# Two RMS norms rewritten: HGRN's root applied behind its projections, the final norm's weights applied during the down units

## The chip, the cores and the metric

One core of a Trainium2 chip runs the whole program. The metric is the device time of one execution in microseconds (us), here the median of a few runs. One execution was also taken by the hardware profiler, which is where the rows further down come from. Matmuls of TensorE (PE) are issued one behind the other; a PE that is busy in every slice is the bound of that slice.

## The reference

The input x is 512 tokens by 1024 features. Block one: `h = x`; HGRN2 mixer, feed-forward (FFN), dilated attention, FFN, each behind an RMS norm and added to h; block two: a sparse attention and gated linear attention mixer, FFN, and a last norm. What the change touches:

```python
def rmsnorm(x, gain):
    y = x * lax.rsqrt(jnp.mean(x * x, axis=-1, keepdims=True) + NORM_EPS)
    return y * gain

u = rmsnorm(h, norm_mix[0])
q, f, i, g = split(u @ w_in)            # four projections for each of 8 heads
forget = lb + (1 - lb) * sigmoid(f);  key = 1 - forget;  query = silu(q);  value = i
...                                     # chunked recurrence, decays from log(forget)
o = rmsnorm(o, out_gain) * silu(g)
...
return rmsnorm_2(x, norm_final)
```

The root `rsqrt(...)` is one number for each token, so `(x * gain * root) @ w` is the same as `((x * gain) @ w) * root`.

## The kernel before, in words

**Layout.** Activations are feature-major: h is eight chunks of 128 features by 512 tokens, float32. The input of a section is split into a rounded high part and a low part (`us`, u_split), as are the weights (`ws`, w_split), and a unit of projection is 24 matmuls: eight chunks by three products (high by high, low by high, high by low, lines 383 to 385), into one PSUM bank.

**Weights.** SP's DMA queue brings each unit's weights into a ring of 4 slots (line 306 for the first four, line 316 later, each when the unit four places earlier has been used). ScalarE (ACT) rounds them into one of 2 slots of w_split (`hi`, line 1013), which it can do once PE has used the unit two places earlier, and GpSimd (POOL) makes the low part (`lo`, line 1495). PE's unit waits for that low part. So each engine's queue, written out by hand, sets when weights are ready: a `hi` that stands behind a waiting instruction comes late.

**The start.** SP loads x (line 298), then gains and ones (line 300), then four units of weights, then the other constants. ACT squares the eight chunks (line 1024), VectorE (DVE) adds the squares (line 1713), PE sums them over the partitions with a matrix of ones (lines 396 and 398, `mean_square`), ACT makes the root from Ln and Exp (lines 1084 and 1086, `rms`). Then DVE multiplies each chunk by gain and root (line 1700), ACT rounds it (line 1034), and POOL (even chunks, line 1504) and DVE (odd chunks, line 1694) make the low part. PE's unit 0 follows that chunk by chunk. Units 0 to 3 are f, q, g, i of head 0, units 4 and 5 are f and q of head 1. Then head 0 begins with its transposes (line 533).

**A head.** ACT takes the sigmoids of f, q and g straight from PSUM (`hgrn_sigmoid`, line 1153) and copies i (`hgrn_value`, line 1161). DVE makes forget, key and query (`hgrn_gates`, lines 1923 to 1927; the query product reads q from PSUM), and silu of g (line 1931, from PSUM). ACT's Ln (line 1157), DVE's scan (line 1826) and the differences of levels (lines 1835, 1836, 1841) lead to ACT's Exp (`decay_exps`, line 1125) and POOL's products with keys and queries (`decayed`, lines 1564, 1565, 1558), between which POOL makes the low parts of the weights of two units. While PE works on one head, the other engines prepare the next, and PE's projections for the next heads are placed between its score matmuls. `FREED` names the semaphore by which a projection's bank becomes free. At a head's end DVE multiplies the output by gain and gate (line 1881), and, after ACT's root for that head, by the root (line 1893).

**The end.** After the last FFN's down units (h is updated on DVE, lines 1771 and 1774) the sum of squares goes as at the start; then `norm(7)` has DVE multiply the eight chunks by gain and root (line 1700) and ACT issues a DMA for each (line 1483).

## Time and profile before

| | |
|---|---|
| runs | 2269.19, 2271.11, 2276.2 us; median 2271.11 |
| the profiled execution | 2268.27 us; span of the core 2266.5 us |
| mean granted clock of PE | 0.987 of full speed |
| busy, share of the span | PE 96%, DVE 44%, ACT 39%, POOL 52% |
| DMA | 193.30 MB, mean 85 GB/s |

The span is 1.8 us shorter than the execution's own time. PE's share is high in nearly all of 40 slices of the page; the first slice is the exception (4 tenths, granted clock 8 tenths), and a smaller one is the last (7 tenths). A timeline row gives the start, the duration, the engine, the line, the operation, what it writes and reads, a count where rows are merged, and in brackets how long the engine sat idle before it and what released it.

### The profile page before, as it was taken

To read this page: it belongs to the slowest core of one execution; us is meant where nothing else is said; L and a number is where in the kernel's file an instruction comes from. 1 tells how busy PE (TensorE), PEld (TensorE's weight loads), DVE (VectorE), ACT (ScalarE), POOL (GpSimd) and SP (SyncE) were. 2 spreads that over 40 slices of the span, in tenths; PEclk is the share of its full clock that TensorE was granted. 3 is DMA by queue.
4 is the path that set the end of the run, shared out by engine and by line. 5 is a ranking of instruction groups with operands and counts; after the bars stand their busy time and mean duration, and the time that the engine had idled before them with its cause. 6 is when DMAs were issued, how large, how long until landed. Compare 5 with 4: busy or idle time off the path is not lost. (4 is left out here: it accounts for less than half of the span.)

```text
span 2266.5 us, 28352 instructions
## 1 busy us (share of the span) xinstructions
PE 2180.3 (96%) x10458; PEld 1795.5 (79%) x10458; DVE 1007.2 (44%) x1479; ACT 872.8 (39%) x1237; POOL 1175.6 (52%) x639
## 2 busy tenths in 40 slices
PE   4899999999999999989999999999899999999997
PEld 3788878888888978878888888788656888888886
DVE  5365566431434037754431446442675235422432
ACT  4567754221323223444221333434465234322222
POOL 3877855554565454535554555455113555554552
PEclk8999999999999999999999999999899999999999
DMA  3121213332332322223332332322101223332331
GB/s 135 56 65 56 74 47 93 93 109 86 95 108 85 93 85 67 72 70 102 94 112 83 93 107 88 123 63 90 56 14 51 95 93 93 100 110 80 101 104 72
DMA packets 53254, 193.30 MB, mean 85 GB/s; under 512 B 6816, under 2 KB 7728, under 8 KB 52912
## 3 DMA queue, kind: packets, MB, share of 16 engines
q1 hardware_dynamic: 50688, 184.95, 26.1%
q10 hardware_dynamic: 2480, 7.19, 0.8%
q8 instruction: 56, 0.92, 0.2%
q14 instruction: 30, 0.25, 0.0%
HBM read 187.92 MB, written 4.19 MB: 85 GB/s over the span
## 5 line engine op out<-in xcount | busy, mean ns | idle before, releaser
L1495 POOL TENSOR_TENSOR w_split<-ring,w_split 128x1024 fp32r<-128x1024 f32 (+3 forms) x327 | 842.9, 2578 | 857.1 <-ACT w_split L1013 857.1
L1013 ACT CAST w_split<-ring 128x1024 fp32r<-128x1024 f32 (+3 forms) x327 | 356.4, 1090 | 1018.2 <-PE ps L385 882.8
L383 PE MATMUL ps<-u_split,w_split 128*128 128x512 f32 x1768 | 705.8, 399 | 22.5 <-POOL w_split L1495 9.7
L385 PE MATMUL ps<-u_split,w_split 128*128 128x512 f32 x1768 | 693.3, 392 | 0.0
L384 PE MATMUL ps<-u_split,w_split 128*128 128x512 f32 x1768 | 692.9, 392 | 0.0
L383 PEld LDWEIGHTS ps<-u_split,w_split 128*128 128x128 f32 x1768 | 334.9, 189 | 102.0 <-issue 19.9
L385 PEld LDWEIGHTS ps<-u_split,w_split 128*128 128x128 f32 x1768 | 334.6, 189 | 71.5
L384 PEld LDWEIGHTS ps<-u_split,w_split 128*128 128x128 f32 x1768 | 335.0, 189 | 68.3 <-issue 1.2
L383 PE MATMUL ps<-hid,w_split 128*128 128x512 f32 x648 | 254.5, 393 | 4.2 <-DVE arena L1975 2.8
L384 PE MATMUL ps<-hid,w_split 128*128 128x512 f32 x648 | 253.3, 391 | 0.0
L385 PE MATMUL ps<-hid,w_split 128*128 128x512 f32 x648 | 253.1, 391 | 0.0
L1790 DVE TENSOR_TENSOR arena<-arena 128x512 f32<-128x512 f32 x66 | 161.9, 2454 | 66.1 <-ACT arena L1101 66.1
L1788 DVE TENSOR_TENSOR arena<-ps,rs_norm 128x512 f32<-128x512 f32 x66 | 45.6, 691 | 261.2 <-PE ps L385 239.2
L383 PEld LDWEIGHTS ps<-hid,w_split 128*128 128x128 f32 x648 | 122.4, 189 | 30.6 <-DVE arena L1975 3.2
L385 PEld LDWEIGHTS ps<-hid,w_split 128*128 128x128 f32 x648 | 122.3, 189 | 25.5
L384 PEld LDWEIGHTS ps<-hid,w_split 128*128 128x128 f32 x648 | 122.4, 189 | 25.4 <-issue 0.2
L1771 DVE TENSOR_TENSOR arena<-arena,ps 128x512 f32 x28 | 19.3, 688 | 187.5 <-PE ps L385 187.5
L1564 POOL TENSOR_TENSOR arena<-arena 128x256 f32<-128x256 f32 x70 | 62.5, 893 | 48.2 <-ACT arena L1125 48.2
L1531 POOL TENSOR_TENSOR hid<-arena,hid 128x512 f32 (+1 forms) x66 | 85.2, 1291 | 4.2 <-ACT hid L1105 4.2
L474 PEld LDWEIGHTS ps<-arena 128*128 128x128 f32 (+1 forms) x672 | 80.5, 190 | 6.7 <-issue 3.7
L1794 DVE TENSOR_TENSOR arena<-ps,rs_norm 128x512 f32<-128x512 f32 x66 | 45.6, 691 | 80.9 <-PE ps L385 80.9
L474 PE MATMUL ps<-arena 128*128 128x64 f32 (+1 forms) x672 | 81.4, 271 | 0.0
(297 smaller groups left out, 2535.6 us busy)
## 6 DMA issues: line engine op xcount, KB each, us to landing
ring<-in_w_hgrn SPq DMA_DIRECT2D x32, 512.0 KB, 3.6
ring<-in_w_attn_qk SPq DMA_DIRECT2D x24, 512.0 KB, 3.5
ring<-in_w_merge SPq DMA_DIRECT2D x24, 512.0 KB, 3.2
ring<-in_w_gu0a SPq DMA_DIRECT2D x22, 512.0 KB, 3.5
ring<-in_w_gu0b SPq DMA_DIRECT2D x22, 512.0 KB, 3.6
ring<-in_w_gu1a SPq DMA_DIRECT2D x22, 512.0 KB, 3.5
ring<-in_w_gu1b SPq DMA_DIRECT2D x22, 512.0 KB, 3.5
ring<-in_w_gu2a SPq DMA_DIRECT2D x22, 512.0 KB, 3.5
```

What stands on the lines that cost most here:

```text
L383: nc.tensor.matmul(ps[:, bank], ws[:, 0, r, w], act[:, 0, c], start=c == 0, stop=False)
L384: nc.tensor.matmul(ps[:, bank], ws[:, 0, r, w], act[:, 1, c], start=False, stop=False)
L385: m = nc.tensor.matmul(ps[:, bank], ws[:, 1, r, w], act[:, 0, c], start=False, stop=c == n - 1)
L474: m = nc.tensor.matmul(ps[:, 4 + n % 2, at:at + C // 2], dv[rows, l, t], later_half, start=True, stop=True)
L1013: nc.scalar.copy(ws[:, 0, slot, 0:w], ring[:, r, 0:w]).then_inc(s["w_hi"], 1)
L1495: nc.gpsimd.tensor_tensor(ws[:, 1, slot, 0:w], ring[:, r, 0:w], ws[:, 0, slot, 0:w].bitcast(F32), ALU.subtract).then_inc(s["w_lo"], 1)
L1531: nc.gpsimd.tensor_tensor(dst, gtmp[:, j % 2], src.bitcast(F32), ALU.subtract).then_inc(s["g_lo"], 1)
L1564: nc.gpsimd.tensor_tensor(x[:, :, 0], x[:, :, 0], kk[:, :, 0], ALU.mult)
L1771: nc.vector.tensor_tensor(hj, hj, ps[:, base + j], ALU.add).then_inc(s["h_ready"], 1)
L1788: nc.vector.tensor_tensor(gnorm[:, x], ps[:, 2 * x], rs[:], ALU.mult).then_inc(s["gate_norm"], 1)
L1790: nc.vector.tensor_tensor(sgate[:, x], sgate[:, x], gnorm[:, x], ALU.mult).then_inc(s["gate_silu"], 1)
L1794: nc.vector.tensor_tensor(gtmp[:, x], ps[:, 2 * x + 1], rs[:], ALU.mult).then_inc(s["up_norm"], 1)
```

## The change

- **Loads.** Gains and the logits of the lower bound come first, then unit 0's weights, then x with one semaphore for each pair of chunks, then ones, the next three units of weights, and the other constants.
- **HGRN's input.** `first_norm` on ACT and `first_input` on DVE make the high part as `h * gain` (ACT, Copy with a scale) and the low part as `h * gain - high` (DVE), without the root, and the squares in between. POOL has no part in it. PE runs unit 0 before the sum of squares.
- **The root.** `hgrn_raw` on DVE multiplies each projection in PSUM by the root (`rs`) and writes it to SBUF: four products a head, 32 in all. Sigmoids then read SBUF; the query and silu products have two SBUF operands; ACT's copy of i is gone. A projection's bank is free after `hgrn_raw`.
- **Places in a head.** The sigmoid of g moves to the head's start on ACT, silu behind the first level on DVE (`prepare(1)`, not `prepare(0)`), and the raw products stand at a head's end on DVE.
- **The last norm.** `last_input` on DVE makes `h * gain` for all chunks and the square of the last chunk during the down units (into `h_gained`); `last_norm` multiplies by the root in five products (1, 1, 2, 2 and 2 chunks), each with one DMA.
- Several semaphores are merged (for example four `mix_*` into `mix_steps`), with the same waits.

```diff
-            for c in range(DC):
-                sp.dma_start(h[:, c], a["x"][:, c]).then_inc(s["x_loaded"], 16)
-            for dst, name in constants[:2]:
-                sp.dma_start(dst[:], a[name]).then_inc(s["norm_consts"], 16)
...
+                    for dst, const in constants[:2]:
+                        sp.dma_start(dst[:], a[const]).then_inc(s["norm_consts"], 16)
+                    sp.dma_start(ring[:, 0, 0:width], w[0]).then_inc(w_ready[0], 16)
+                    for c in range(DC):
+                        sp.dma_start(h[:, c], a["x"][:, c]).then_inc(s[f"x_loaded{c // 2}"], 16)
+                    sp.dma_start(ones[:], a["ones"]).then_inc(s["norm_consts"], 16)
+                    for k in range(1, RING):
...
-            FREED = ("sig_f", "query", "silu_g", "vf_ready")
+            FREED = ("raw_f", "raw_q", "raw_g", "vf_ready")
...
-            pe.wait_ge(s["norm_consts"], 32)
+            hgrn_project(0, 0, ready=u_chunk(0))
+            pe.wait_ge(s["norm_consts"], 16 * 3)
             mean_square(0)
-            for k in range(4):
-                hgrn_project(0, k, ready=None if k else u_chunk(0))
+            for k in range(1, 4):
+                hgrn_project(0, k)
...
+            def first_norm():
+                act.wait_ge(s["norm_consts"], 16 * 2)
+                hi("hgrn", 0)
+                for c in range(DC):
+                    act.wait_ge(s[f"x_loaded{c // 2}"], 16 * 2)
+                    nc.scalar.activation(us[:, 0, c], h[:, c], ACT.Copy, scale=gains[:, 0, c:c + 1]).then_inc(s["u_hi"], 1)
+                    if c >= 4:
+                        act.wait_ge(s["sq_sum"], max(c - 4, 1))
+                    nc.scalar.activation(nsq[:, c % 4], h[:, c], ACT.Square).then_inc(s["sq_ready"], 1)
+                hi("hgrn", 1)
+                hi("hgrn", 2)
+                rms(0)
...
+            def first_input(c):
+                dve.wait_ge(s["u_hi"], c + 1)
+                nc.vector.scalar_tensor_tensor(out=us[:, 1, c], in0=h[:, c], scalar=gains[:, 0, c:c + 1],
+                                               in1=us[:, 0, c].bitcast(F32), op0=ALU.mult, op1=ALU.subtract
+                                               ).then_inc(s["u_lo_odd"] if c % 2 else s["u_lo_even"], 1)
+                if c >= 2:
+                    add_square(0, c - 1)
...
+            def hgrn_raw(head, done, bank, dst):
+                unit = (1, 0, 2, 3).index(bank)
+                dve.wait_ge(s["w_used"], cnt(head, 4, FIRST["hgrn"] + unit + 1))
+                nc.vector.tensor_tensor(dst, ps[:, bank], rs[:], ALU.mult).then_inc(s[done], 1)
...
-            lo("hgrn", 0)
-            norm(0, "hgrn")
-            lo("hgrn", 2)
-            lo("hgrn", 3)
-            hgrn_decayed(0, {4: lambda: lo("hgrn", 4), 8: lambda: lo("hgrn", 5)})
-            lo("hgrn", 6)
+            for k in range(5):
+                lo("hgrn", k)
+            hgrn_decayed(0, {2: lambda: lo("hgrn", 5), 5: lambda: lo("hgrn", 6)})
             lo("hgrn", 7)
...
+            def last_input(n, j):
+                if j == DC - 1:
+                    dve.wait_ge(s["h_ready"], h_done(NORM_AFTER[n], j))
+                    nc.vector.tensor_tensor(nsq[:, 3], h[:, j], h[:, j], ALU.mult).then_inc(s["sq_ready"], 1)
+                for c in {4: (0, 1), 5: (2, 3), 6: (4, 5), 7: (6, 7)}[j]:
+                    dve.wait_ge(s["h_ready"], h_done(NORM_AFTER[n], c))
+                    nc.vector.tensor_scalar(h_gained[:, c], h[:, c], gains[:, n, c:c + 1], None, ALU.mult
+                                            ).then_inc(s["u_tmp"], 1)
```

The order on ACT in the start, from the squares to the weights of unit 5. Before (`arena` with `128x1024` and `128x1536` are the decays, `w_split` is a `hi`):

```order
L1084 ACTIVATE rs_norm<-ps,small 128x512
L1086 ACT_TABLE_LOAD
L1086 ACTIVATE rs_norm<-rs_norm 128x512
L1034 CAST u_split<-arena 128x512 x4
L1013 CAST w_split<-ring 128x1024
L1034 CAST u_split<-arena 128x512 x4
L1153 ACT_TABLE_LOAD
L1153 ACTIVATE arena<-ps 128x512
L1013 CAST w_split<-ring 128x1024
L1153 ACTIVATE arena<-ps 128x512
```

and now:

```order
L1020 CAST w_split<-ring 128x1024 x2
L1093 ACT_TABLE_LOAD
L1093 ACTIVATE rs_norm<-ps,small 128x512
L1095 ACT_TABLE_LOAD
L1095 ACTIVATE rs_norm<-rs_norm 128x512
L1172 ACTIVATE arena<-arena 128x24
L1020 CAST w_split<-ring 128x1024
L1160 ACT_TABLE_LOAD
L1160 ACTIVATE arena<-arena 128x512 x2
L1169 ACT_TABLE_LOAD
L1169 ACTIVATE arena<-arena 128x512
L1020 CAST w_split<-ring 128x1024
```

The weights of units 1 and 2 are rounded ahead of the root, those of unit 3 ahead of the sigmoids, those of unit 4 behind Ln.

DVE from one head's end to the next head's scan, in the loop over heads. Before:

```order
L1881 SCALAR_TENSOR_TENSOR arena<-ps,small,arena 128x512 [waits o_sq,o_lo]
L1892 REGISTER_ALU [waits o_scaled]
L1893 TENSOR_TENSOR arena<-arena 128x512 [waits o_rstd]
L1853 REGISTER_ALU
L1854 TENSOR_TENSOR arena<-ps,ident_sb 128x512 [waits score_ps]
L1944 REGISTER_ALU
L1931 TENSOR_TENSOR arena<-arena,ps 128x512 [waits sig_g,scores]
```

and now, up to the same place:

```order
L1893 TENSOR_TENSOR arena<-ps,rs_norm 128x512 [waits w_used]
L1878 SCALAR_TENSOR_TENSOR arena<-ps,small,arena 128x512 [waits o_sq,silu_g,o_lo]
L1892 REGISTER_ALU [waits o_scaled]
L1893 TENSOR_TENSOR arena<-ps,rs_norm 128x512 [waits w_used]
L1892 REGISTER_ALU
L1893 TENSOR_TENSOR arena<-ps,rs_norm 128x512 [waits w_used]
L1886 ISA [waits o_scaled]
L1887 TENSOR_TENSOR arena<-arena 128x512 [waits o_rstd]
L1892 REGISTER_ALU
L1893 TENSOR_TENSOR arena<-ps,rs_norm 128x512 [waits w_used]
L1849 REGISTER_ALU
L1850 TENSOR_TENSOR arena<-ps,ident_sb 128x512 [waits score_ps]
```

Four products with the root (now line 1893) stand around the head's output, and the silu product has left the place behind line 1850.

## Rows read from the trace of the kernel before

**Rows 1.** Windows: busy us of engines, PEclk, DMA share, GB/s in a stretch.
```profile
54.00:56.00 2.00, 1.86 (x5) 1.50 (x6) 2.00 (x7) 0.59 (x1) 0.09 (x1) 0.60 0.21 84
93.00:118.00 25.00, 25.00 (x139) 21.30 (x138) 11.62 (x19) 19.14 (x24) 23.46 (x20) 1.00 0.27 85
```
**Rows 2.** Source line 298, the loads of x.
```profile
DMA to landing us min/median/max: 2.9/4.1/5.5
```
**Rows 3.** Timeline, the start up to the end of unit 0.
```profile
9.62 1.28 ACT L1024 ACT_TABLE_LOAD   x1 [9.62 <-DMA arena<-in_x]
10.92 4.27 ACT L1024 ACTIVATE arena<-arena 128x512 f32<-128x512 f32 x8
...
15.09 1.03 ACT L1013 CAST w_split<-ring 128x1024 fp32r<-128x1024 f32 x1
...
16.93 2.05 PE L396 MATMUL ps<-arena,ones_sb 128*128 128x512 f32 x2 [16.93 <-DVE arena L1713]
...
23.24 2.08 DVE L1700 SCALAR_TENSOR_TENSOR arena<-arena,gains_sb,rs_norm 128x512 f32<-128x512 f32 x3 [4.25 <-ACT rs_norm L1086]
...
26.59 0.77 PE L383 MATMUL ps<-u_split,w_split 128*128 128x512 f32 x1 [6.05 <-POOL u_split L1504]
...
40.19 0.60 ACT L1153 ACTIVATE arena<-ps 128x512 f32<-128x512 f32 x1 [1.39 <-PE ps L385]
```
**Rows 4.** Timeline, units 2 to 5 and the start of head 0.
```profile
50.73 1.22 DVE L1826 TENSOR_TENSOR_SCAN arena<-reset_sb,arena 128x512 f32<-128x512 f32 x1
51.45 2.64 POOL L1495 TENSOR_TENSOR w_split<-ring,w_split 128x1024 fp32r<-128x1024 f32 x1 [7.25 <-ACT w_split L1013]
...
54.14 0.58 PE L383 MATMUL ps<-u_split,w_split 128*128 128x512 f32 x1 [2.74 <-POOL w_split L1495]
...
56.64 3.30 POOL L1564 TENSOR_TENSOR arena<-arena 128x256 f32<-128x256 f32 x1 [2.55 <-ACT arena L1125]
...
58.65 0.68 DVE L1841 TENSOR_TENSOR arena<-arena 128x512 f32<-128x512 f32 x1
...
67.17 0.77 PE L383 MATMUL ps<-u_split,w_split 128*128 128x512 f32 x1 [5.68 <-POOL w_split L1495]
...
75.15 1.28 POOL L1558 TENSOR_TENSOR arena<-arena 128x512 f32<-128x512 f32 x1
75.33 0.47 PE L383 MATMUL ps<-u_split,w_split 128*128 128x512 f32 x1 [0.43 <-POOL w_split L1495]
...
80.88 0.60 PE L533 MATMUL ps<-ident_sb,arena 128*128 128x128 f32 x4
...
94.63 0.48 ACT L1205 COPY arena<-ps 128x384 f32<-128x384 f32 x1 [1.03 <-PE ps L546]
```
**Rows 5.** Page, costliest groups: busy us, mean ns of one | idle before.
```profile
L1790 DVE TENSOR_TENSOR arena<-arena 128x512 f32<-128x512 f32 x66 | 161.9, 2454 | 66.1 <-ACT arena L1101 66.1
L1788 DVE TENSOR_TENSOR arena<-ps,rs_norm 128x512 f32<-128x512 f32 x66 | 45.6, 691 | 261.2 <-PE ps L385 239.2
```
**Rows 6.** Timeline of POOL and of PE, inside the loop over heads.
```profile
157.91 0.77 POOL L1564 TENSOR_TENSOR arena<-arena 128x256 f32<-128x256 f32 x1 [6.47 <-ACT arena L1125]
...
172.28 2.38 POOL L1495 TENSOR_TENSOR w_split<-ring,w_split 128x1024 fp32r<-128x1024 f32 x1
...
173.88 1.02 PE L500 MATMUL ps<-arena,ones_sb 128*128 128x512 f32 x2
```
**Rows 7.** Timeline, the last norm.
```profile
2253.18 0.68 DVE L1713 TENSOR_TENSOR arena<-arena 128x512 f32<-128x512 f32 x1
...
2253.91 1.13 PE L396 MATMUL ps<-arena,ones_sb 128*128 128x512 f32 x2 [1.38 <-DVE arena L1713]
...
2254.88 1.02 PE L398 MATMUL ps<-arena,ones_sb 128*128 128x512 f32 x2
...
2258.60 5.39 DVE L1700 SCALAR_TENSOR_TENSOR arena<-arena,gains_sb,rs_norm 128x512 f32<-128x512 f32 x8 [4.74 <-ACT rs_norm L1086]
2259.38 4.98 ACTq L1483 DMA_DIRECT2D out_h<-arena  x8
```

More of the change, by code:

```diff
@@ L1013, in hi, with last_norm @@
                 nc.scalar.copy(ws[:, 0, slot, 0:w], ring[:, r, 0:w]).then_inc(s["w_hi"], 1)
[L1015 to L1021 removed]
+            def last_norm(n):
+                for c in range(DC - 1):
+                    act.wait_ge(s["h_ready"], h_done(NORM_AFTER[n], c))
                     if c >= 4:
@@ L1145, in _, with hgrn_sigmoid, hgrn_gate_sigmoids @@
             act.wait_ge(s["credit"], 2)
-            norm(0, "hgrn")
-            def hgrn_sigmoid(head, k, dst, done):
-                src = (1, 0, 2)[k]
-                act.wait_ge(s["w_used"], cnt(head, 4, FIRST["hgrn"] + k + 1))
-                if head != 0 and k:
-                    act.wait_ge(s[("", "query", "silu_g")[k]], cnt(later(head, -1), 1, 1))
-                nc.scalar.activation(dst, ps[:, src], ACT.Sigmoid).then_inc(s[done], 1)
+            first_norm()
+            def hgrn_sigmoid(head, raw, src, dst, done):
+                act.wait_ge(s[raw], cnt(head, 1, 1))
+                nc.scalar.activation(dst, src, ACT.Sigmoid).then_inc(s[done], 1)
+            def hgrn_gate_sigmoids(head):
+                hgrn_sigmoid(head, "raw_f", sf_, sf_, "sig_f")
+                hgrn_sigmoid(head, "raw_q", qry[(head if isinstance(head, int) else head[1]) % 2], sq_, "sig_q")
             def hgrn_log(head):
@@ L1479, in _ @@
             ffn(2, None)
-            norm(7)
-            for c in range(DC):
-                act.wait_ge(s["credit"], 3 + c)
-                act.dma_start(out[:, c], h[:, c]).then_inc(s["stored"], 16)
-            act.wait_ge(s["stored"], 16 * DC)
+            last_norm(7)
+            for n, (lo, hi) in enumerate(LAST_PARTS):
+                act.wait_ge(s["credit"], 3 + n)
+                act.dma_start(out[:, lo:hi], h[:, lo:hi]).then_inc(s["stored"], 16)
+            act.wait_ge(s["stored"], 16 * len(LAST_PARTS))
         @block.gpsimd
@@ L1772, in residual @@
                 for j in range(loops, DC):
+                    for c in {6: (1, 2, 3, 4), 7: (5, 6)}.get(j, ()):
+                        add_square(norm, c)
                     dve.wait_ge(s["w_used"], FIRST[section] + j + 1)
                     nc.vector.tensor_tensor(h[:, j], h[:, j], ps[:, base + j % 2], ALU.add).then_inc(s["h_ready"], 1)
-                    for c in {5: (1, 2, 3), 6: (4, 5), 7: (6,)}.get(j, ()):
-                        add_square(norm, c)
+                    if norm is not None:
+                        last_input(norm, j)
             def ffn(f, norm):
@@ L1819, in _ @@
             nc.vector.memset(start[:, 2:3], 0.0).then_inc(s["o_rstd"], 2)
-            for c in range(1, DC - 1):
-                add_square(0, c)
-            dve.wait_ge(s["norm_consts"], 32)
+            for c in range(DC):
+                first_input(c)
             def cumulate(it, b, log_decay):
@@ L1886, in head_output @@
                     return
-                if head != HEADS_H - 2:
-                    output_rooted(head, r, tmp, dst, done)
             def output_rooted(head, r, tmp, dst, done):
@@ L1962, in hgrn_head @@
                     end_exponents(bcum, dec)
+                    hgrn_raw(nxt, "vf_ready", 3, vf)
                 dve.wait_ge(s["o_lo"], cnt(head, 1, 1))
                 head_output(head, hgain, ors, otmp, sgl, otmp, s["o_full"])
+                if more:
+                    dve.wait_ge(s["o_scaled"], cnt(head, 1, 1))
+                    hgrn_raw(nxt, "raw_g", 2, sgl)
+                if not isinstance(head, int):
+                    hgrn_raw(nxt2, "raw_f", 1, sf_)
+                    output_rooted(head, ors, otmp, otmp, s["o_full"])
+                    hgrn_raw_query(nxt2)
             over_heads(dve, hgrn_head)
@@ L2346, in _ @@
             ffn(2, 7)
-            norm(7, s["credit"])
+            last_norm(7, s["credit"])
 def kernel(**inputs):
```

158 lines of the change are left out of this document (62 added, 96 removed).

## The prediction

> **What bounds the kernel now.** I read the windows first. From the first heads on PE is busy for all of a stretch (25.00 of 25.00 us) at a granted clock of 1.00 [rows 1]: work of DVE, ACT or POOL taken away there is worth nothing, unless it ends a wait of PE. So the edit can only pay in the first 80 us and the last 15 us, and can only hurt by a new wait in between. Next I read the timeline of the start. PE does its first projection matmul at 26.59 us, after x has landed (9.62), eight squares, their sum, a sum over partitions from 16.93, the root, the products and the low parts; unit 0, held up chunk by chunk, is done at 40.19, where the sigmoid that reads it starts [rows 3]. Units 1 to 5 follow with three waits for low parts of weights (2.74, 5.68 and 0.43 us), and head 0 starts at 80.88 [rows 4]. PE's work in these units is small: unit 5 takes 80.88 - 75.33 = 5.55 us at full clock [rows 4]. The clock matters too: right after the idle 2.74 us the granted clock was 0.60 over the stretch 54 to 56 [rows 1]. Unit 3 ran from 54.14 to 61.49 (67.17 less 5.68), 7.35 us, or 1.8 more than unit 5, and unit 4 from 67.17 to 74.90, 7.73 us, or 2.2 more [rows 4]. PE is then at the lower of its two levels, 1.2 GHz, and climbs back to 2.4 after some microseconds of work.
>
> **The change, part by part: the new start.**
> - First work. Unit 0's weights are now the third DMA, issued near 1.7 us. A transfer of x took 2.9 to 5.5 us to land [rows 2]; I take 3.5, so 5.2 us. ACT: table load (1.28) beforehand, rounding 1.03 [rows 3], to 6.3. POOL's low part, 2.4 to 2.6 [rows 4, 6], to 8.8. PE starts at 8.8 and not at 26.59.
> - Pace of unit 0. ACT spends a product (0.6) and a square (4.27 / 8 = 0.53) per chunk, 1.15 us; DVE a low part (2.08 / 3 = 0.69 [rows 3]) and an add (0.68 [rows 7]), 1.4 with gaps. PE at 1.2 GHz needs 3 x 0.427 = 1.28 us a chunk (512 columns at 1.2 GHz). All three end near 19: ACT finishes chunk 7 at 16.6, DVE at 18.6, PE at 19.0. x itself is not the limit: it landed at 9.62 and now has 0.57 MB more ahead of it, about 11, and ACT reaches the last pair at 14.
> - Sum of squares, now behind unit 0: 2.0 us at full clock [rows 7], 3.6 at half, since its first half alone took 2.05 in the start [rows 3]. PE will have worked for 10 us by then, so I take 2.0: 21.0. Its price is new on PE; the root's latency is hidden behind unit 1.
> - Units 1 to 3. The rounding of unit 1 is done at 17.6, its low part at 20.3; unit 2's at 22.7. They run back to back to 26.5, 32.0 and 37.5. Unit 3's rounding waits for the end of unit 1, 26.5, and is ready at 30.1, before 32.0.
> - The log of forget. ACT after that rounding (27.6): table load 1.28, two sigmoids of 0.60 [rows 3], table load, Ln 0.6: 32.0. Unit 4's rounding needs unit 2 done (32.0), so it ends at 33.1, its low part at 35.7 (2.64 [rows 4]), in time for 37.5. Unit 4 ends at 43.0.
> - Unit 5's low part is the late one. DVE's scan to the last difference took 50.73 to 59.33 = 8.6 us [rows 4], so now 32.1 to 40.7. POOL's first decay product was held for 3.30 us, to 59.94, 0.6 behind DVE's last difference [rows 4]; so here it ends at 41.3. Three more halves of 0.72 bring 43.5, and the low part of unit 5, which now stands behind two levels, 45.9. Its rounding, behind ACT's third Exp, is ready before. PE idles 2.9 us and pays 1.8 for the clock as unit 3 did: unit 5 ends at 53.2.
> - Head 0 thus starts at 53.2 instead of 80.88: **-27.7 us**. What it needs next is ready: keys and queries at 31, the value at 42, POOL's decays by 58, while PE's transposes of them were over 94.6 - 80.9 = 13.7 us into the head [rows 4], now 67.
>
> Bounds. Were unit 0's weights to land 2 us later, the sum of squares to take 3.6 and unit 1 to run low (2.2), it is 5.8 us less: -21.9. Were POOL's first product not held, it is up to 2.6 us of idle and 1.8 of clock more: -32.1.
>
> **The heads.** DVE gets four products a head from PSUM: line 1788 is the same form and takes 0.691 us, so 32 x 0.69 = 22 us, of which DVE's idle time takes all as long as nothing PE waits for is behind them. ACT loses the copy of i and two table loads a head, worth nothing while PE is busy. The products at a head's end wait for projections that PE has issued before the matmul that DVE's next step needs, so they hold nothing up. The tight place is elsewhere: POOL's second low part ends at 172.28 + 2.38 = 174.66, and PE, whose two ones-matmuls start at 173.88 and take 0.86 together, needs it at about 174.75 [rows 6]: 0.1 us of slack. That chain starts with Ln, which now stands behind a third sigmoid (0.6), and with the scan, which stands behind silu (0.69); against this ACT has lost a copy and two table loads on the way there, about 0.4 us of it before the sigmoids by my estimate. I take 0; the upper bound is 0.65 x 6 heads = +4 us. A gain is excluded, since PE has no idle time there.
>
> Two products change sides, though: query and silu read PSUM before and now have two SBUF operands. Line 1790, with two SBUF operands beside a busy POOL, takes 2.454 us; line 1788, with one, 0.691 [rows 5]. At the place where query and silu stand (some 4 us into a head) POOL waits for the decays, 6.47 us in all [rows 6], so I price them at 0.7 each. The Trainium skill (SBUF — State Buffer, "SBUF: two separate sides") says that VectorE instructions with two SBUF inputs and GpSimd's share a port pair as an exclusive lock for the whole instruction. By it the raw products, with one SBUF input, cost POOL nothing, and the two moved ones can wait for a whole low part; the trace agrees in the two means. It is the mechanism of the slower rival.
>
> **The end.** Now: DVE's last add (2253.18, 0.68), then four matmul halves from 2253.91 to 2255.9, then the root [rows 7]. In the change the adds are over before the last update, so the first pair of halves (1.0) runs before it, and DVE's square of chunk 7 (0.68) takes the place of the add; only the second pair follows: **-1.0 us**. The last products take 2 x 0.67 + 3 x 1.21 = 5.0 instead of 5.39 [rows 7], but the eight transfers, issued from 2259.38 and landed at 2266.5 (2.1 MB in 7.1 us), already keep pace with DVE; I count 0 of that 0.4. Bounds -1.4 and 0. The gain products (0.6 each) lie beside down units of over 7 us.
>
> **Sum.** 2268.27 - 27.7 + 0 - 1.0 = 2239.6 against the profiled execution. The median of the runs shown is 2.8 us above it, which would make 2242.4. I take **2241**. A change of this kernel's time can be told from none beyond 0.3%, or 6.8 us.
>
> **The rivals.**
> 1. *Part of it is given back.* The start comes in at the upper bounds, and the loop slips by half a microsecond a head. For it: 0.1 us of slack [rows 6], and the clock, which fell after only 2.74 us of idle. Against it: in each head PE's other waits have microseconds of slack. 2241 + 5.8 + 4 gives up to 2251.
> 2. *The start was covered anyway.* If head 0, reached early, waits for POOL's decays, the gain moves from the norm to there. POOL took 76.4 - 56.6 = 19.8 us for them [rows 4]; from 37.9 that is 57.7, while PE needs them at 66. To eat the gain, POOL would have to be some 30 us later. The same goes for late loads. 2262 or more.
> 3. *Slower: query and silu queue behind POOL.* If both are held as line 1790 is, each costs 2.454 - 0.69 = 1.76 us more; with 0.6 of the third sigmoid and 0.69 of the moved silu the scan is 4.8 us later in every head, POOL's decays with it, and PE waits 4.7 us for a low part in 6 to 7 heads, each time with 1.8 for the clock: 6.5 x 7 = 45 us, 2241 + 45 = 2286. It makes the kernel slower by 0.3% from about 4 us of delay a head. Against it: POOL's 6.47 us without work at this place of every head [rows 6].
>
> **How the numbers follow.** My forecast 0.78, rival 1 0.13, rival 2 0.04, rival 3 0.05. The first two are faster by over 0.3%, and some 0.01 of the second rival: faster 0.92, same 0.03, slower 0.05. The forecast's own bounds are 2241 - 4.4 - 0.4 = 2236 and 2241 + 5.8 + 1 = 2248; with rival 1, and 2 us for the spread between runs, the range is 2234 to 2252.
>
> **What would show it.** Right: PE's first projection matmul near 9 us, unit 0 over by 20, one wait of about 3 us before unit 5, head 0 (line with the transposes) near 53; no idle time of PE inside the loop; only two matmul halves between the last update and Ln. Wrong: an idle row of PE before the second low part of a head, releaser POOL, in every head (rival 1 or, if over 4 us, 3); query or silu products at about 2 us; a wait of PE on POOL's decays in head 0 (rival 2); half clock from 20 to 30 us. If PE's first matmul is not before 15 us, the step on the loads is wrong.

## The result, and the profile after

| | before | after |
|---|---|---|
| runs, us | 2269.19, 2271.11, 2276.2, 2277.68 | 2245.87, 2254.36, 2254.52, 2254.84 |
| median, us | 2273.65 | 2254.44 |
| the profiled execution, time / span, us | 2268.27 / 2266.5 | 2254.36 / 2252.6 |
| mean granted clock, profiled execution | 0.987 | 0.987 |
| busy: PE, DVE, ACT, POOL | 96, 44, 39, 52% | 97, 46, 38, 52% |

The ratio (of the means) is 0.9906, with a 95% interval from 0.9883 to 0.9929: the kernel is faster, by some 19 us between the medians and 21 us between the means. Before now has a fourth run (2277.68), which the forecast did not have. One later run of before, 2787.31 us at a granted clock of 0.745, is left out of all comparisons below. The forecast was 2241 us (2234 to 2252), so the direction was right and the size was not; the result is above the range.

Where the two profiled executions part is read best from the times at which PE reaches the same place in both:

| PE reaches | before | after | gained so far |
|---|---|---|---|
| transposes of head 0 | 80.88 | 53.38 | 27.5 |
| transposes of head 1 | 114.01 | 90.05 | 24.0 |
| first lone matmul of the output units | 321.58 | 300.32 | 21.3 |
| last norm, the ones-matmuls behind the last chunk | 2253.91 | 2240.79 | 13.1 |
| end of the span | 2266.5 | 2252.6 | 13.9 |

So 27.5 us were gained by head 0, 3.5 given back in head 0, 2.7 in the later heads, 8.1 in the 1940 us behind them, which the change does not touch, and 0.8 gained at the end. A "lone" matmul is the first one behind the heads that waits for POOL's product of the output units (line 521 before, 527 after); it marks the end of all that the start and the heads do.

**The start** came nearly as worked out. The timeline of after, from the first unit's weights to head 0 (start, duration, engine, line, operation; idle before it and its releaser):

```profile
6.75 1.04 ACT L1020 CAST w_split<-ring 128x1024 fp32r<-128x1024 f32 x1
7.87 2.35 POOL L1496 TENSOR_TENSOR w_split<-ring,w_split 128x1024 fp32r<-128x1024 f32 x1 [7.41 <-ACT w_split L1020]
10.91 0.77 PE L389 MATMUL ps<-u_split,w_split 128*128 128x512 f32 x1 [10.91 <-DVE u_split L1705]
...
19.27 1.02 PE L402 MATMUL ps<-arena,ones_sb 128*128 128x512 f32 x2
...
21.31 0.50 PE L389 MATMUL ps<-u_split,w_split 128*128 128x512 f32 x1 [0.16 <-POOL w_split L1496]
...
38.62 3.29 POOL L1556 TENSOR_TENSOR arena<-arena 128x256 f32<-128x256 f32 x1 [2.56 <-ACT arena L1134]
...
46.44 0.77 PE L389 MATMUL ps<-u_split,w_split 128*128 128x512 f32 x1 [3.07 <-POOL w_split L1496]
...
53.38 0.60 PE L539 MATMUL ps<-ident_sb,arena 128*128 128x128 f32 x4
```

PE starts at 10.9 instead of 26.59 [rows 3], unit 0 is over before the sum of squares at 19.27, that sum is over at 21.15, and the three waits of [rows 4] are down to one of 3.07 us (and one of 0.16), behind POOL's product that DVE held for 3.29 us.

**Head 0** is 36.67 us long and not 33.13. The timeline of after, POOL, DVE and then PE (the scan, a DVE row, among them):

```profile
55.13 0.84 POOL L1557 TENSOR_TENSOR arena<-arena 128x256 f32<-128x256 f32 x1
55.93 2.55 POOL L1550 TENSOR_TENSOR arena<-arena 128x512 f32<-128x512 f32 x2
58.43 2.37 POOL L1496 TENSOR_TENSOR w_split<-ring,w_split 128x1024 fp32r<-128x1024 f32 x1
...
56.79 4.29 DVE L1924 TENSOR_SCALAR arena<-arena 128x512 f32<-128x512 f32 x1 [1.19 <-ACT arena L1160]
...
63.34 1.22 DVE L1822 TENSOR_TENSOR_SCAN arena<-reset_sb,arena 128x512 f32<-128x512 f32 x1
...
63.50 2.00 PE L480 MATMUL ps<-arena 128*128 128x64 f32 x16 [0.88 <-DVE arena L1862]
...
75.88 1.15 PE L498 MATMUL ps<-arena 128*128 128x128 f32 x8 [1.25 <-DVE arena L1871]
```

DVE's forget product (L1924, for head 1) takes 4.29 us, where it takes 1.03 in a later head. It ends when POOL's queue of two products and the low part of unit 7 is through. The scan then starts 9.96 us into head 0 and not 6.98 as in a later head (below), 3.0 us late, and head 0 is 2.9 us longer than a later head. Two waits of PE on DVE follow (0.88 and 1.25 us), and one of 0.42 on a low part as in every later head. The granted clock was 1.00 over all of head 0, so none of it is the clock's.

**The later heads** take 33.74 us each, before 33.24, and each has one idle row of PE. PE and DVE of after, one head:

```profile
123.80 0.60 PE L539 MATMUL ps<-ident_sb,arena 128*128 128x128 f32 x4
...
151.96 0.50 PE L389 MATMUL ps<-u_split,w_split 128*128 128x512 f32 x1 [0.49 <-POOL w_split L1496]
...
127.40 1.03 DVE L1924 TENSOR_SCALAR arena<-arena 128x512 f32<-128x512 f32 x1 [1.37 <-ACT arena L1160]
...
130.78 1.23 DVE L1822 TENSOR_TENSOR_SCAN arena<-reset_sb,arena 128x512 f32<-128x512 f32 x1
```

It is the low part of [rows 6]. The scan starts 6.98 us into the head; before it was 153.53 - 147.06 = 6.47. It is also the sign that the prediction had named for rival 1: an idle row of PE before the second low part of a head, releaser POOL, in every head. (The expectations below say 6.27, from a head start read 0.2 us late.)

**The end** is as forecast but for 0.2 us: from the ones-matmuls at 2240.79 to the end of the span 11.8 us, before 12.6 [rows 7]. (Counted from the last matmul of the down units, at 2252.14 before and 2238.90 after, it is 0.7 and not 0.8.) DVE's last products, five in 4.70 us:

```profile
2240.05 0.69 DVE L1680 TENSOR_TENSOR arena<-arena 128x512 f32<-128x512 f32 x1
...
2240.79 1.13 PE L404 MATMUL ps<-arena,ones_sb 128*128 128x512 f32 x2 [0.65 <-DVE arena L1680]
...
2244.62 4.70 DVE L1691 TENSOR_TENSOR arena<-arena,rs_norm 128x512 f32<-128x512 f32 x5 [3.08 <-ACT rs_norm L1095]
```

### The profile page after: what moved, and what is told of

The parts are those of the page before. It is cut to its first block and busy times, and to the rows that moved or that the text cites. A ratio compares the mean times of both kernels' runs of the same rounds, so it can differ in the third digit from the quotient of the medians.

```text
span 2252.6 us, 28350 instructions
## 1 busy us (share of the span) xinstructions
PE 2183.4 (97%) x10458; PEld 1794.9 (80%) x10458; DVE 1036.7 (46%) x1513; ACT 848.7 (38%) x1213; POOL 1169.6 (52%) x635
## 5 line engine op out<-in xcount | busy, mean ns | idle before, releaser
L1766 DVE TENSOR_TENSOR arena<-arena,ps 128x512 f32 x28 | 19.3, 688 | 187.5 <-PE ps L391 187.5
```

The lines of the kernel that those rows point to most:

```text
L1766: nc.vector.tensor_tensor(hj, hj, ps[:, base + j], ALU.add).then_inc(s["h_ready"], 1)
```

## The experiments

All but one start from the changed kernel. The edits are shown shortened: names are abbreviated, and the conditions for the last heads and the waits that follow from a move are left out. Times of the whole kernel turned out to spread by up to 12 us within the runs of one kernel, so the edits are read from PE's timeline. "Period" is the mean of heads 2 to 5; "lone" is the start of the first lone matmul of the output units, the sum of all that happened up to there. In the three executions of the changed kernel (after, a_same, a_same2) the period repeats to 0.02 us and head 0 to 0.23, but the start of head 0 lies between 53.38 and 54.25, and lone with it between 300.32 and 301.03. That start depends on the clock in unit 5, behind the wait of 3.07 us: in a_v2lo1, whose edits all lie in the loop over heads, it was 0.70 from 49.00 to 54.80 and head 0 starts at 54.83; in after it was 0.96 from 49.00 to 53.40. A late start makes head 0 look short, since POOL's queue is through at about the same time either way, so "head 0 at" and "head 0 takes" are to be added. Differences of lone under 0.7 us show nothing.

| run | head 0 at | head 0 takes | period | lone | median, us |
|---|---|---|---|---|---|
| before | 80.88 | 33.13 | 33.24 | 321.58 | 2273.65 |
| after | 53.38 | 36.67 | 33.73 | 300.32 | 2254.44 |
| a_same | 53.62 | 36.51 | 33.74 | 300.49 | 2249.43 |
| a_same2 | 54.25 | 36.44 | 33.74 | 301.03 | 2257.24 |
| a_lo1 | 53.57 | 35.77 | 33.69 | 299.86 | 2251.64 |
| a_silu | 53.68 | 39.21 | 33.67 | 304.61 | 2255.65 |
| a_lo7 | 53.69 | 36.25 | 33.73 | 300.19 | 2254.37 |
| a_v2 | 53.97 | 36.49 | 33.77 | 300.93 | 2255.00 |
| a_v2lo1 | 54.83 | 34.04 | 33.71 | 299.51 | 2246.54 |
| a_lo5 | 49.29 | 38.39 | 33.75 | 298.01 | 2253.38 |
| a_hi3 | 53.26 | 36.31 | 34.27 | 302.74 | 2257.85 |
| a_hi3lo1 | 54.84 | 34.02 | 34.22 | 302.73 | 2257.89 |
| a_best | 54.05 | 33.94 | 34.58 | 304.11 | 2254.65 |
| a_best5 | 49.24 | 37.14 | 34.58 | 302.39 | 2249.41 |
| a_nosilu | 53.50 | 36.03 | 33.24 | 297.35 | 2248.51 |
| a_v2lo15 | 49.24 | 37.26 | 33.73 | 297.20 | 2251.98 |
| a_gps | 53.78 | 36.04 | 33.27 | 297.76 | 2247.43 |
| a_gps5 | 49.50 | 38.01 | 33.24 | 295.40 | 2244.81 |
| a_gps57 | 49.26 | 38.00 | 33.24 | 295.14 | 2244.73 |

### The same kernel again: the clock

No edit.

> The changed kernel once more, nothing edited. Theory A (the shortfall of 14.7 us is 3.5 us in head 0, 2.8 us in the loop over heads, both the same in every execution, and 7.8 us of low granted clock in the last attention stage, 1650 to 1710 us, that comes and goes between executions): the times fall in two groups some 8 us apart, 2246 and 2254, with granted clocks of 0.993 and 0.987. Rival B (the low clock there belongs to the change, since it moves that stage by 21 us): all executions near 2254, clock 0.987, and 2245.87 was a single stray.

> The changed kernel once more, beside the two others on the same chip. Start and heads to within 0.3 us as before (first lone output matmul at 300.4), the time between 2245 and 2257 by the granted clock alone.

Times 2245.67, 2248.51, 2250.35 and 2256.7 us at mean clocks of 0.993, 0.989, 0.990 and 0.986, and later 2246.67 at 0.992 and 2255.6 to 2258.76 at 0.986 or 0.987. So the time follows the clock, but not in two groups, and the low clock is not tied to one place. The profiled execution of a_same is level with that of after to 0.2 us up to the lone matmul, is 2.1 us ahead of it at 1450, lies 6.9 us behind it from 1500 us on, and gains 4.6 of that back in the last attention stage. Windows of after, then of a_same (busy us of PE, PEld, DVE, ACT and POOL, granted clock, DMA share, GB/s):

```profile
1460.00:1490.00 30.00, 29.10 (x153) 23.97 (x153) 17.30 (x37) 7.44 (x15) 18.09 (x13) 0.94 0.22 67
...
1650.00:1660.00 10.00, 8.02 (x39) 4.14 (x37) 5.75 (x10) 4.48 (x13) 2.55 (x1) 0.68 0.01 2
1690.00:1710.00 20.00, 17.09 (x118) 10.84 (x118) 14.11 (x33) 10.75 (x33) 3.20 (x2) 0.74 0.00 1
```
```profile
1460.00:1490.00 30.00, 29.82 (x105) 24.25 (x106) 9.90 (x25) 3.71 (x8) 12.74 (x12) 0.61 0.10 23
...
1650.00:1660.00 10.00, 7.83 (x54) 4.25 (x52) 9.52 (x18) 5.77 (x16) 2.56 (x1) 0.88 0.17 52
1690.00:1710.00 20.00, 15.57 (x126) 9.84 (x126) 16.61 (x36) 13.13 (x36) 3.76 (x2) 0.91 0.00 1
```

At 1460 PE is busy (29.8 of 30 us) behind an idle time of 0.88 us in a_same and 0.90 in after, and runs at 0.61 in the one execution and 0.94 in the other. In the profiled execution of before it runs at 1.00 there, behind the same 0.88 us, and the stretches that answer to 1650 and 1690 ran at 1.00 too:

```profile
1481.00:1511.00 30.00, 29.12 (x161) 24.29 (x161) 17.41 (x37) 8.08 (x15) 19.07 (x13) 1.00 0.23 70
...
1671.00:1681.00 10.00, 8.57 (x60) 4.83 (x62) 7.51 (x14) 5.19 (x16) 2.34 (x1) 1.00 0.01 2
1711.00:1731.00 20.00, 18.22 (x148) 12.40 (x149) 12.74 (x32) 12.93 (x32) 2.53 (x2) 1.00 0.01 2
```

That is where the 8.1 us went between the two profiled executions: 7.8 us were lost between 1602 and 1707 us of after. The rest is smaller stretches of both signs. Right behind the lone matmul, for one, PE idled 2.83 us before and 2.81 after, and then ran at 0.55 over the next 7 us in before and at 1.00 in after, which gave after 2.8 us; it lost 3.0 of them again by 960. The same kernel, run again, has the low clock elsewhere or for a shorter time, so it is not a cost of the change. The prediction was made against an execution of 2268.27, which is among the fastest of before: of the 11 runs beside a_same, the median is 2275.64 and the fastest 2271.08. Between the means of before and of the changed kernel lie 21.1, 25.0 and 17.2 us in the three rounds that timed it (after, a_same and a_same2).

### One wait of PE in each head taken away: the low part earlier

```diff
-hgrn_decayed(nxt, {4: lo(unit(nxt2, 0)), 7: lo(unit(nxt2, 1))})
+hgrn_decayed(nxt, {4: lo(unit(nxt2, 0)), 6: lo(unit(nxt2, 1))})   # POOL
-decay_exps(nxt, dec, 3); hi(unit(nxt2, 1))
+hi(unit(nxt2, 1)); decay_exps(nxt, dec, 3)                        # ACT
```

> POOL's second low part of each head goes one decay level earlier, ACT's rounding with it. Theory A (PE waits 0.3 to 0.5 us in each head because this low part ends too late): these waits are gone from all heads, head period 33.25 instead of 33.74, 2.8 to 3.5 us less by the start of the output units (300.3 to about 297). Rival C (the period is longer because DVE and ACT have more work per head, and the wait only moves): the period stays at 33.7, with PE idle elsewhere in the head, most likely before the transposes of the decayed keys or the outputs.

Theory A fell: the waits on the low part are gone, and a wait on DVE's chain of states (L1874) of 0.31 to 0.64 us stands in their place; the period is 33.69. So another wait stood less than 0.1 us behind the one that PE had shown, and not microseconds.

```profile
143.33 0.93 PE L498 MATMUL ps<-arena 128*128 128x128 f32 x6 [0.31 <-DVE arena L1874]
```

### Silu moved: to the end of the head before, and behind the chain of states

```diff
-hgrn_sigmoid(head, "raw_g", sgl, sg_, "sig_g")     # a_silu alone: ACT, beside the sigmoids of f and q
+hgrn_sigmoid(nxt, "raw_g", sgl, sg_, "sig_g")      # a_silu: behind state_exps(nxt)
-if n == 1: hgrn_silu(head)                         # DVE, ahead of the scan
+hgrn_silu(nxt)     # a_silu: behind hgrn_raw(nxt, "raw_g")
+hgrn_silu(head)    # a_v2: ahead of head_output; and ACT: hgrn_log(nxt) ahead of the copy of vT
```

> The sigmoid and the product of the output gate go to the end of the head before, away from the scan. Theory A (the scan starts 6.98 us into a head and not 6.27, since ACT's third sigmoid and DVE's silu stand ahead of it, and POOL and the low part follow 0.7 us later): the scan is back at about 6.3, PE's waits of 0.3 to 0.5 us are gone, 2.8 to 3.5 us less by the output units. If only one of the two (ACT or DVE) mattered or neither, the scan stays near 6.9 and the waits stay. The extra table load (1.28) lies in 2.8 us of ACT idle time and costs nothing.

> In the loop over heads DVE's silu product goes behind the chain of states (just ahead of the head's output), and ACT takes Ln ahead of the copy of the value; nothing else. Theory A (the head period is 33.74 and not 33.25 because the scan starts at 6.98 us of a head and not at 6.27, delayed by silu (0.68) on DVE and by the third sigmoid (0.58) on ACT at the same place): the scan starts near 6.3 us, POOL's decays follow, PE's waits in the heads go or shrink under 0.1 us, head 1 to the first lone output matmul takes 207.6 instead of 210.3 us. Rival C (the period follows from another chain, such as POOL's own load): the scan comes earlier and the period stays at 33.7.

> The same, and POOL's second low part of a head one decay level earlier. Theory A: as the run before, or 0.1 us a head less if silu, now beside POOL's products, delays that low part; no idle time of PE inside the loop after head 0. Rival C: the period stays at 33.7.

a_v2lo1 is a_v2 with the edit of a_lo1. In none of them does the period change (33.67, 33.77, 33.71), though forget to scan went from 3.38 us to 2.90 in a_v2. Silu has two SBUF operands. At the end of the head before it waited for POOL's low part, 2.60 us instead of 0.68, and ahead of head 0, where POOL's queue is unbroken, 6.92 us, which made head 0 2.5 us longer:

```profile
54.49 6.92 DVE L1933 TENSOR_TENSOR arena<-arena 128x512 f32<-128x512 f32 x1
...
185.97 2.60 DVE L1933 TENSOR_TENSOR arena<-arena 128x512 f32<-128x512 f32 x1 [1.03 <-ACT arena L1160]
```

Behind the chain of states silu itself took 0.68 us, but the product of POOL beside it 1.25 instead of 0.73, and POOL's stretch from first product to last low part 22.1 us instead of 21.6. What was taken out ahead of POOL came back inside it. DVE and POOL of a_v2:

```profile
145.51 0.68 DVE L1933 TENSOR_TENSOR arena<-arena 128x512 f32<-128x512 f32 x1
145.54 1.25 POOL L1558 TENSOR_TENSOR arena<-arena 128x256 f32<-128x256 f32 x1
```

Head 0 of a_v2lo1 takes 34.04 us, but it starts 1.4 us late, for the clock; head 1 starts at 88.87 instead of 90.05, so at most 1.2 us are the edit's.

### POOL's queue at head 0

```diff
-lo("hgrn", 7)                                  # a_lo7
+pool.wait_ge(s["query"], 2); lo("hgrn", 7)
-hgrn_decayed(0, {2: lo("hgrn", 5), 5: ...})    # a_lo5; and ACT: hi("hgrn", 5) behind decay_exps(0, dec, 0)
+hgrn_decayed(0, {0: lo("hgrn", 5), 5: ...})
```

> In head 0 POOL takes the low part of unit 7 only when the next head's query is there. Theory A (DVE's forget product of head 0 took 4.29 us since POOL's two products and this low part held it back, and PE's idle 0.88 and 1.25 us in head 0 follow): forget at about 1.9 us, head 0 about 34.5 us long instead of 36.7, 2 us less. Rival D (POOL's low part holds DVE wherever it stands): another DVE row of head 0 grows by 2 us, head 0 stays at 36.5.

> POOL takes the low part of unit 5 ahead of the decay products, so PE's wait of 3.07 us before unit 5 goes. Theory A (head 0 is bound by POOL's backlog and DVE behind it, so whatever PE saves before head 0 is given back in it): head 0 starts 3 to 5 us earlier, near 49, and head 1 starts where it did, 90.0 +- 0.7. Rival E (PE's time at head 0 counts in full, the 3.5 us lost in head 0 are a fixed cost of the collision): head 1 starts at 85 to 87.

a_lo7 did as rival D said. Forget is down from 4.29 to 1.78 us, and silu, the next product with two SBUF operands, up from 0.68 to 2.76, beside the same low part. Timeline of a_lo7, DVE and POOL:

```profile
57.09 1.78 DVE L1925 TENSOR_SCALAR arena<-arena 128x512 f32<-128x512 f32 x1 [1.19 <-ACT arena L1160]
...
60.20 2.76 DVE L1933 TENSOR_TENSOR arena<-arena 128x512 f32<-128x512 f32 x1
...
60.02 2.39 POOL L1496 TENSOR_TENSOR w_split<-ring,w_split 128x1024 fp32r<-128x1024 f32 x1 [1.42 <-DVE arena L1929]
```

In a_lo5 the wait of 3.07 us before unit 5 shrank to 0.35 and head 0 starts 4.1 us earlier, but takes 1.7 us more: neither theory in full. PE there waits 2.34 us for DVE's levels, and DVE's and POOL's products lengthen each other (DVE's take 0.77 to 2.59 us from 52.70 to 63.48). POOL's backlog gives back somewhat under half of what PE gains ahead of it.

### ACT's rounding out of the way

```diff
-hi(unit(nxt2, 3))           # ACT, ahead of the sigmoids of the next head
+hi(unit(nxt, 3))            # behind hgrn_log(nxt)
```

a_hi3lo1 adds the edit of a_lo1, a_best those of a_lo1 and a_v2, a_best5 that of a_lo5 too.

> ACT's rounding of a head's last unit (1.04 us) goes from just ahead of the sigmoids to just behind Ln; nothing else. Theory F (the head period of 33.74 is the length of a ring of waits through all engines, from PE's outputs over ACT's Ln, Exp, rounding, sigmoid, DVE's forget, scan, level differences and chain of states to the next outputs; PE's own work is 33.25, and shortening PE's or POOL's part alone moved the wait but not the period): 1.04 us less of ring puts it under PE's 33.25, so the heads from 1 on take 33.25 us and PE's idle time in them is gone, 3 us less by the first lone output matmul; in head 0 up to 1 us more. Rival G (the period is set by DVE's or POOL's amount of work, each unchanged here): period stays at 33.7.

> The same with POOL's second low part one decay level earlier. Theory F: period 33.25 as in the run before, no idle time of PE inside the loop. Rival G: 33.7 with PE's wait at the outputs.

> The rounding behind Ln, silu behind the chain of states, Ln ahead of the value's copy, the second low part earlier. Theory F: period 33.25 (PE's own work, it can't be less), and in head 0, where neither the low part of unit 7 nor silu stands ahead of forget and scan, 34.0 to 35 us instead of 36.7: first lone output matmul at 296 or earlier instead of 300.3. Rival G: 299.

> The same, with the low part of unit 5 ahead of the decay products. As in the run with this edit alone, which brought head 1 from 90.05 to 87.68, half of the 4.1 us that head 0 starts earlier are kept: first lone output matmul 2 to 4 us earlier than in the run before, time near 2241 where the granted clock is 0.99. Rival: POOL's backlog takes all of it, same as the run before.

A miss of both theories: the period became longer, 34.27. Forget came 1.0 us earlier in a head, as meant. But POOL's low part of that unit now runs right beside DVE's level differences and holds the first of them 1.90 us instead of 0.42. Timeline of a_hi3, POOL and DVE:

```profile
130.73 2.53 POOL L1495 TENSOR_TENSOR w_split<-ring,w_split 128x1024 fp32r<-128x1024 f32 x1 [4.93 <-ACT w_split L1020]
...
131.64 1.90 DVE L1830 TENSOR_TENSOR arena<-arena 128x256 f32<-128x256 f32 x1
```

In the ring of the next section forget's part is 0.94 us shorter and the part behind forget 1.48 longer, which is the 0.54 us of the period. The runs with more edits inherit this (34.22 and 34.58), where a_best was expected at 33.25. a_best5 was expected near 2241 us at a clock of 0.99; its run at 0.992 took 2247.81.

### The ring, and a link taken out of it

These misses fit a ring of waits, from POOL over DVE and ACT back to POOL, that is longer than PE's own 33.24 us. From after, one turn: POOL's unbroken stretch from 135.18 to 156.75 (21.57); DVE's rooted product of the head, ready at 155.67 but ended at 157.30 behind POOL's last low part (0.55); ACT's two roundings, table load and sigmoid up to DVE's forget at 161.14 (3.84); forget, Ln, scan, two levels and their Exp up to POOL's next stretch at 168.91 (7.77). Sum 33.73. In before the same four are 21.60, 0.60, 3.80 and 7.24, sum 33.24.

The sums alone prove nothing, since rows that go once round a head always add up to the period. What counts is that each part starts where the one ahead ends, and that only the last part differs, by 0.53 us. Before, the rooted product started at 179.42, 0.09 us ahead of the end of POOL's last low part, so the ring had at most some 0.1 us of slack beside PE's own work.

In the last part two products stand ahead of the scan that did not stand there before: ACT's third sigmoid ahead of Ln, and silu on DVE. Ln ends at 164.39 and DVE is free at 164.53; the scan starts at 164.51. So either of the two alone would have held it, and no run takes them apart. Rows of after (one turn), then of before:

```profile
135.18 0.77 POOL L1556 TENSOR_TENSOR arena<-arena 128x256 f32<-128x256 f32 x1 [7.04 <-ACT arena L1134]
...
154.37 2.38 POOL L1496 TENSOR_TENSOR w_split<-ring,w_split 128x1024 fp32r<-128x1024 f32 x1
...
155.67 1.63 DVE L1887 TENSOR_TENSOR arena<-arena 128x512 f32<-128x512 f32 x1 [4.33 <-ACT arena L1152]
...
161.14 1.02 DVE L1924 TENSOR_SCALAR arena<-arena 128x512 f32<-128x512 f32 x1 [1.37 <-ACT arena L1160]
...
163.76 0.63 ACT L1169 ACTIVATE arena<-arena 128x512 f32<-128x512 f32 x1
164.09 0.44 DVE L1862 COPY_PREDICATED arena<-lvl_mask_sb,ps 128x256 f32<-128x256 uint32 x1
164.51 1.23 DVE L1822 TENSOR_TENSOR_SCAN arena<-reset_sb,arena 128x512 f32<-128x512 f32 x1
...
168.91 0.77 POOL L1556 TENSOR_TENSOR arena<-arena 128x256 f32<-128x256 f32 x1 [7.03 <-ACT arena L1134]
```
```profile
177.12 2.39 POOL L1495 TENSOR_TENSOR w_split<-ring,w_split 128x1024 fp32r<-128x1024 f32 x1
...
179.42 0.69 DVE L1893 TENSOR_TENSOR arena<-arena 128x512 f32<-128x512 f32 x1 [6.29 <-ACT arena L1143]
...
183.91 1.05 DVE L1923 TENSOR_SCALAR arena<-arena 128x512 f32<-128x512 f32 x1 [0.65 <-ACT arena L1153]
...
191.15 0.77 POOL L1564 TENSOR_TENSOR arena<-arena 128x256 f32<-128x256 f32 x1 [6.47 <-ACT arena L1125]
```

The run that takes the link out leaves the output gate's sigmoid and silu away and multiplies by the raw gate, so its output is another; only its times are read.

```diff
-hgrn_sigmoid(head, "raw_g", sgl, sg_, "sig_g")
-if n == 1: hgrn_silu(head)
```

> The changed kernel without the output gate's sigmoid (ACT) and silu product (DVE) in the heads; the raw gate is used in their place, so this part of the result is left out. Theory H (the head period is a ring: POOL's unbroken stretch of 21.57 us, then DVE's rooted product, which waits 0.9 us for POOL's last low part to end, ACT's two roundings, table load and sigmoid, DVE's forget, Ln, scan and first differences, and POOL's first product again; a product of DVE with two SBUF operands adds its 0.7 us wherever in the ring it stands, by itself or by lengthening POOL's stretch): 0.69 less, the ring is under PE's own 33.25, period 33.25, no idle time of PE in heads 1 to 5. Rival I (moving or removing one product changes nothing since another wait of about the same length stands behind it): 33.6 to 33.7.

Period 33.24, no idle time of PE in heads 1 to 5, lone 3.0 us earlier. The ring holds, the second wait of equal length does not. The run takes out sigmoid and silu together.

The next run joins the edits of a_lo5, a_v2 and a_lo1.

> Low part of unit 5 first, silu behind the chain of states, Ln ahead of the value's copy, second low part one level earlier. By Theory H the period stays at 33.74, but head 0 starts at 49.3 and takes 37 us or less: first lone output matmul between 296.5 and 298, 3 us before the changed kernel, and the time 3 us under it where the clock is the same.

It came as expected, 297.20 with a period of 33.73. The medians of a_nosilu, a_v2lo15 and a_same2, timed side by side (2248.51, 2251.98, 2257.24), stand in the right order, but runs of one kernel spread as far.

### Silu with one operand from PSUM

```diff
-hgrn_raw(nxt, "raw_g", 2, sgl);        nc.vector.tensor_tensor(sgl, sg_, sgl, ALU.mult)
+hgrn_raw(nxt, "raw_g", 2, ps[:, 2]);   nc.vector.tensor_tensor(sgl, sg_, ps[:, 2], ALU.mult)
-FREED = ("raw_f", "raw_q", "raw_g", "vf_ready")
+FREED = ("raw_f", "raw_q", "silu_g", "vf_ready")
```

with the sigmoid and silu at the places of a_silu (for head 0 silu stands one product earlier); a_gps5 adds the edit of a_lo5, a_gps57 that of a_lo7 too.

> The raw output gate stays in its PSUM bank (scaled in place), its sigmoid and silu go to the end of the head before, so silu reads one operand from PSUM as it did in the kernel before the change. Theory H (a product with two SBUF operands waits for POOL or makes POOL wait, and so adds 0.7 us to the ring wherever it stands): this one does neither, silu about 0.7 us (2.6 and, before head 0, 6.9 in the run that did the same with both operands in SBUF), period 33.25, first lone output matmul near 297. Rival I: 33.7, as after every other move of silu.

> The same with the low part of unit 5 first: head 0 starts 4 us earlier and takes some 2 us longer, first lone output matmul near 295, 5 us before the changed kernel; time near 2248 at a clock of 0.987 and near 2241 at 0.993.

> The same, with the low part of unit 7 behind the next head's query. With silu gone from that place no row of DVE with two SBUF operands stands right behind it but the scan: if the scan is not held, head 0 is 0.5 to 2 us shorter than in the run before (near 293 to 294.5); if POOL's low part then holds the scan or the first differences, as it held silu before (2.76 us), no gain.

The same move that was worth nothing in a_silu now gives a period of 33.27 and lone 2.6 us earlier. DVE of a_gps: silu is not held, beside the same low part, and the rooted product is held less, as it is no longer late by the ring:

```profile
148.58 0.69 DVE L1933 TENSOR_TENSOR arena<-arena,ps 128x512 f32<-128x512 f32 x1 [0.99 <-ACT arena L1160]
...
154.95 1.14 DVE L1888 TENSOR_TENSOR arena<-arena 128x512 f32<-128x512 f32 x1 [4.33 <-ACT arena L1152]
```

a_gps57 has no gain over a_gps5, and could have none: POOL reaches the low part of unit 7 at 60.21, long after the query product that its edit waits for (over at 56.1). In both runs that low part holds a level difference for 2.60 us. DVE of a_gps5:

```profile
60.71 2.60 DVE L1833 TENSOR_TENSOR arena<-arena 128x256 f32<-128x256 f32 x1
```

Both have the earliest lone of the study, 5 us ahead of the changed kernel. Their ratios to before are 0.9879 (0.9860 to 0.9899) for a_gps57 and 0.9884 (0.9865 to 0.9903) for a_gps5, but a_same, with no edit at all, has 0.9881 (0.9866 to 0.9895). So that step is shown on PE's timeline, not by the times.

### The last norm alone

The kernel before, with the change's last norm and nothing else of it.

> The kernel before, with only the last norm of the change. Forecast of the prediction: 1.0 us from PE's last ones-matmuls on (12.6 us from there to the end of the span before). From the two traces: 11.8 against 12.6, 0.8 less. Rival: the parts help nothing and it is 12.6 again. In the time of the whole kernel this can't be seen.

From the ones-matmuls behind the last chunk (2262.14) to the end of the span (2273.9) 11.8 us, before 12.6: 0.8 less. The median, 2275.87, beside 2276.28 can't show it, as expected.

## Why the prediction was wrong

- **The new start: right.** Forecast -27.7 us, measured -27.5. First matmul 10.9 and not 8.8: DVE's first low part was held for 2.29 us beside POOL's. That it cost nothing is in part luck: PE was forecast at half pace for all of unit 0, and its matmuls were 0.43 us apart only up to 14.9 and then 0.23, so it caught up with DVE, whose pace of 1.26 us a chunk set the end at 19.3. The sum of squares took 1.9 us at full clock (2.0 forecast), the idle time before unit 5 was 3.07 (2.9), and head 0 started at 53.4 (53.2).
- **"What it needs next is ready": the first step that failed.** POOL's decays were over at 58.5 (58 forecast), and PE did not wait for them. But DVE works for head 1 while PE works on head 0, and its forget product stood behind that queue of POOL. The step looked at what PE needs of head 0, and not at what DVE needs meanwhile. Of the 3.5 us of head 0 some 3.0 are this (the scan 2.98 us later than in a later head), and 0.5 are the next step's. No run removes the 3.0 by itself: in a_lo7 forget was freed and the same low part held silu instead (36.25 for 36.67). a_lo5 shows it as a rate: of 4.1 us gained ahead of head 0, 1.7 are given back in it.
- **"I take 0; the upper bound is 0.65 x 6 heads": the second.** The slack of 0.1 us and the mechanism were right, the value was at the other end: 0.5 us a head, 2.7 in all. The 0.4 us that ACT was to save "before the sigmoids by my estimate" had no row behind it and did not come: from the end of the rooted product to forget it was 3.80 us before and 3.84 after, since ACT waits for that product in both, and its copy and table loads had stood ahead of this wait. The waits that PE showed were taken as single ones with "microseconds of slack" behind them. They are one ring, and before the change it was within 0.1 us as long as PE's own work. Rival 1 had this mechanism; it gave it 0.13.
- **"I price them at 0.7 each": right in place, incomplete.** The query product took 0.68 us and silu 0.68 in the later heads; rival 3, which has them wait for POOL there, did not come. But at the two other places tried, silu with two SBUF operands cost as much or more: it waited 2.60 us itself (a_silu) or made POOL's stretch 0.5 us longer (a_v2).
- **The end: right** in mechanism, 0.8 for 1.0.
- **The sum.** -27.5 + 3.5 + 2.7 - 0.8 = -22.1 us is the change's own worth. Against 2268.27 it would be 2246.2, where the runs at the higher clocks lie (2245.67 to 2246.67). The remaining 8.1 us of the profiled execution are the clock's: the largest single part of the 14.8 us between the prediction's sum (2239.6) and that execution (2254.36). The prediction allowed 2 us for the spread between runs, from three runs of before; the runs of before lie between 2268.02 and 2281.28. That stretch less 22.1 is 2246 to 2259, which is the range that the failed steps mended would have left.

## What to carry to other kernels

Where several engines work one step ahead of PE, add up one turn of the ring of waits through all of them, beside PE's own work of that step: if the two are equal, a product put into the ring costs time in every turn (here 0.5 us for a silu of 0.68 on DVE with a sigmoid of 0.58 on ACT), and taking away the wait that PE shows only shows the next one. When a stage starts earlier, ask of each engine, and not of PE alone, what is still in its queue and what it shares with its neighbour. Where DVE must work beside a busy POOL, try one operand from PSUM before a better place: here it gave back 0.47 us a head, where the moves gave 0.07 at most. And compare places in PE's timeline before whole times, when the clock moves the time by more than the edit.

## What the hardware showed

- DVE and POOL kept each other out for whole instructions, both ways. A product of 0.68 us took 6.92 behind an unbroken queue of POOL, and a product of POOL of 0.73 took 3.29 behind a run of DVE's. The Trainium skill (SBUF — State Buffer, "SBUF: two separate sides") has an exclusive lock for DVE operations with two SBUF inputs, and also for those "in a 2-port perf mode". The prediction took the first condition only. Forget is a tensor_scalar with one tensor operand and was held for 4.29 us, so the second matters too, as far as this row can tell; no run here separates it. The key product (L1926), also a tensor_scalar with one operand in SBUF, took 0.43 us where nothing held it and 0.95 beside POOL in a_lo5.
- A tensor_tensor of DVE (128x512) with one operand in PSUM took 0.67 to 0.72 us in every row of every trace, whatever POOL did: the raw products, and silu in a_gps. A predicated copy with its source in PSUM and its mask in SBUF (L1862) is another matter: 0.43 us free and 0.75 beside POOL's products (136.64 in after).
- The granted clock falls to the lower of its levels, 1.2 GHz, behind idle times of about 1 us in some executions and hardly or not in others (0.61, 0.94 and 1.00 over 30 us from the same place, behind 0.88 to 0.90 us of idle time). Runs of one kernel differ by up to 12 us with it. What decides it was not found.
